# A hybrid SSD, sparse-attention and mixture-of-experts step on one core: squares after the gates, attention in double steps, and a reworked residual stage

## The reference

```python
h = rmsnorm(x, norm_g);  proj = h @ w_in          # z, xBC, dt, q, k, v, indexer, two gates
y_ssd = ssd_scan(silu(causal_conv(xbc)), ...)     # 4 groups of heads, chunks of 64
y_ssd = rmsnorm(y_ssd * silu(z), ssm_norm_g)      # its squares are summed over all 2048 channels
branch_a = y_ssd @ w_ssm_out
o = dsa_attention(q, k, v, indexer ...)           # 16 heads, 2 KV heads; scores masked to the top keys
branch_b = o @ w_attn_out
x = x + (sigmoid(g0) * branch_a + sigmoid(g1) * branch_b) @ w_o      # the residual stage
h = rmsnorm(x);  group and expert logits -> 2 experts of one group of 8, out of 32
for e in range(32):
    he = silu(h @ w1[e]) * (h @ w3[e]);  y += combine[:, e] * (he @ w2[e])
out = rmsnorm(x + y)
```

## Time and profile before

| | us |
|---|---|
| runs: median (lowest to highest) | 1581.36 (1580.76 to 1584.17) |
| the profiled execution | 1584.12 |
| its span, first to last instruction | 1582.5 |
| PE busy, DVE, ACT, POOL | 1428.0, 659.1, 470.7, 177.9 |
| from the end of `ga` (688.5) to the first scores (734.8) | 46.3 |
| prompt attention (734.8 to the first scores of the running streams, 826.45) | 91.65 |
| last x1 half read (1258.2) to the first expert's transposes (1290.87) | 32.6 |
| first to last scatter of the experts' results (1308.3 to 1547.2) | 238.9 |

### The profile page before, as it was taken

The page is one execution under the profiler, slowest core; times in us unless marked ns, Lnnn a source line. Parts: engine busy times, 40 slices in busy tenths (PEclk is TensorE's granted clock), DMA queues, the critical chain, the costliest instruction groups (busy, mean ns, idle before and its releaser), DMA issues.

```text
span 1582.5 us, 19000 instructions
## 1 busy us (share of the span) xinstructions
PE 1428.0 (90%) x7458; PEld 893.7 (56%) x7458; DVE 659.1 (42%) x1467; ACT 470.7 (30%) x1059; POOL 177.9 (11%) x270
## 2 busy tenths in 40 slices
PE   7999999999999999979988899999999949878780
PEld 5545654754754745756555677777765535544440
DVE  3059952775785785602755521000023523211105
ACT  2161025643643743413765500000002111111112
POOL 3000000310221221220000000000000013222210
PEclk9999999999999999988999999999999959999986
DMA  7721314423523423525008520212033199999975
GB/s 230 217 80 29 107 54 122 160 98 93 171 87 106 158 87 102 161 99 149 15 14 170 148 110 0 106 53 53 20 136 128 56 381 394 415 415 416 414 292 206
DMA packets 135180, 247.43 MB, mean 156 GB/s; under 512 B 38836, under 2 KB 81572, under 8 KB 126164
## 3 DMA queue, kind: packets, MB, share of 16 engines
q1 hardware_dynamic: 124020, 215.10, 39.8%
q0 software_dynamic: 11072, 31.12, 5.5%
HBM read 216.50 MB, written 36.88 MB: 160 GB/s over the span
## 4 chain that ended last, share of the span: by engine, by line
PE 82%; ACT 5%; DVE 5%; DMA 4%; issue 3%; POOL 1%; SPq 1%; DVEq 0%; ACTq 0%; POOLq 0%
PE psum L1262 49%; PE psum L1536 8%; PE psum L1266 5%; PE psum L1440 4%; PE psum L1552 3%; ACT arena L1721 2%; PE psum L1294 2%; PE psum L1182 1%; ACT arena L1798 1%; PE psum L1172 1%; PE psum L1247 1%; DMA x_rows<-oT 1%; PE psum L1075 1%; DVE arena L2423 1%; PE psum L1211 1%
## 5 line engine op out<-in xcount | busy, mean ns | idle before, releaser
L1262 PE MATMUL psum<-hT,wring 128*128 128x512 f32 (+2 forms) x2176 | 597.1, 436 | 0.4 <-issue 0.4
L1262 PEld LDWEIGHTS psum<-hT,wring 128*128 128x128 f32 x2176 | 350.3, 192 | 237.3 <-issue 197.1
L1266 PE MATMUL psum<-ident,arena 128*128 128x128 f32 (+3 forms) x950 | 143.1, 288 | 40.3 <-DMA arena<-x_rows,src_row 16.9
L1721 ACT ACTIVATE arena<-psum 128x512 f32<-128x512 f32 (+9 forms) x199 | 106.8, 578 | 204.7 <-PE psum L1262 138.0
L1266 PEld LDWEIGHTS psum<-ident,arena 128*128 128x128 f32 (+3 forms) x950 | 106.6, 145 | 98.2 <-issue 78.1
L1262 PE MATMUL psum<-arena,wring 128*128 128x320 f32 x512 | 138.1, 431 | 0.0
L1262 PEld LDWEIGHTS psum<-arena,wring 128*128 128x128 f32 x512 | 96.6, 189 | 41.2
L1536 PE MATMUL psum<-wring,arena 128*64 128x256 f32 x608 | 78.7, 417 | 25.2 <-issue 20.1
L1536 PEld LDWEIGHTS psum<-wring,arena 128*64 128x64 f32 x608 | 51.4, 151 | 48.0 <-issue 29.1
L2430 DVE TENSOR_TENSOR arena<-psum,arena 128x128 f32<-128x128 f32 x32 | 9.3, 292 | 161.3 <-ACT arena L1865 152.6
L2359 DVE TENSOR_TENSOR arena<-psum,arena 128x320 f32<-128x320 f32 x16 | 7.9, 491 | 156.1 <-PE psum L1262 156.1
(11 more groups left out here) (318 smaller groups left out, 1504.8 us busy)
## 6 DMA issues: line engine op xcount, KB each, us to landing
wring<-in_w SPq DMA_DIRECT2D x38, 1024.0 KB
arena<-in_w SPq DMA_DIRECT2D x32, 1024.0 KB
wring<-in_w_in SPq DMA_DIRECT2D x13, 2048.0 KB, 7.9
hT<-in_w SPq DMA_DIRECT2D x14, 1024.0 KB
oT<-in_w SPq DMA_DIRECT2D x12, 1024.0 KB
arena<-a_rows SPq DMA_DIRECT2D x20, 512.0 KB, 4.3
arena<-in_state_ssm SPq DMA_DIRECT2D x16, 512.0 KB, 7.3
out<-arena POOLq DMA_DIRECT2D x16, 512.0 KB, 4.2
```

The source lines that it names most:

```text
L1262: ins = mm(out, chunk[:, k, m0:m0 + m], rhs(k), start=first and k == 0, stop=last and k == ks - 1)
L1266: return nc.tensor.transpose(out, in_, ident[0:rows, 0:rows])
L1721: release(fn(out, in_, ACT.Copy), key)
```

## The change

1. `squares_pe` moves behind `gb`.
2. Prompt attention takes two pairs per step d: scores of 2d and 2d+1, values of the two pairs of step d-2, transposes of the two of step d-1. A transposed head has one bank of a pool of three (4, 5, 6), "o" has bank 7 alone. The multiplication by the reciprocal goes to POOL (64 instructions, L957 of the new file), DVE keeps the reciprocal and copies head 1's transposes (L2087), ACT copies head 0's. `sm` has 8 buffers for 6, `pT` 4 for 2.
3. Residual stage: x is loaded for all five tiles at once, straight into x1, and added in place; `h2T` keeps two tiles and `xn` three, in other memory than oT. So w13(0), w2(0), w13(1) and w13(2) are issued right behind x. After the last x1 half come w2(1), w13(3), w2(2); w13(4), w2(3), w2(4) come when the last router is done, the rows are stored and the first gather has landed. For the last tile, its second transposes and its `scale` stand ahead of the picks of tile 3; ranks and places of tile 3 stand behind the picks of tile 4. The memset of `rows_in` moves up behind the first store.

```diff
@@ def plan_group / ssd_pe
-                    if j == 3:
-                        squares_pe(pe, g)
                 w = wait_chunk(pe, ("wgb", 0))
...
+                squares_pe(pe, g)
@@ def attention_pe
+            for d in range(PAIRS // 2 + 2):
+                for stage, lag in ((scores, 0), (values, 2), (probs_turned, 1)):
+                    for m in (2 * (d - lag), 2 * (d - lag) + 1):
+                        if 0 <= m < PAIRS:
+                            stage(m)
@@ plan_banks
+        if d >= 2 and d % 2 == 0:
+            b.add(("o", (d - 2) // 2), (7,))
+        for a in range(2):
+            if 1 <= d < PAIRS // 2 + 1:
+                for g in range(AKV):
+                    b.add(("pT", 2 * d - 2 + a, g), (4, 5, 6))
@@ POOL
+            for u in range(AKV * PAIRS):
+                w = P * (u // AKV // AR + 1)
+                pool.wait_ge(S["rinv_ready"], u + 1)
+                nc.gpsimd.tensor_tensor(sm[:, u % 8, 0:w], sm[:, u % 8, 0:w],
+                                        rinv[:, u % 8:u % 8 + 1].broadcast_to([P, w]), ALU.mult).then_inc(S["p_scaled"], 1)
@@ attention_dve, per double step, behind four least()
+                for a in range(2):
...
+                            nc.vector.reciprocal(rinv[:, u % 8:u % 8 + 1], rsum[:, u % 8:u % 8 + 1]) \
+                                .then_inc(S["rinv_ready"], 1)
+                    if 0 <= m < PAIRS:
...
+                        release(copy(pT[:, a, 1, 0:w], bank(key)[:, 0:w]), key)
@@ SP
-                sp.dma_start(xres[:, tt % 2, :], src).then_inc(pair["xres_loaded"][tt % 2], 16)
-                if tt == 1:
-                    load13(0)
-                    load13(1)
+                sp.dma_start(x1[:, tt, :], src).then_inc(tile_loaded[tt], 16)
+            load13(0)
+            load2(0)
+            load13(1)
+            load13(2)
             wait_read(sp, ("x1", NT - 1, 1))
-            load2(0)
-            load13(2)
             load2(1)
             load13(3)
             load2(2)
             wait_full(sp, ("rt", NT - 1))
+            rows_stored(sp)
+            sp.wait_ge(gathered_rows[0], 16)
+            load13(4)
             load2(3)
-            sp.wait_ge(S["xn_stored"], 16 * NT)
-            load13(4)
             load2(4)
@@ residual, and the ring of h2T, on DVE
                 release(tt_(x1[:, t, 512 * m:512 * m + 512], bank(("x1", t, m)),
-                            xres[:, t % 2, 512 * m:512 * m + 512], ALU.add), ("x1", t, m))
+                            x1[:, t, 512 * m:512 * m + 512], ALU.add), ("x1", t, m))
+                if t >= 2:
+                    wait_full(dve, ("rt", t - 2))
@@ the last tile on DVE (PE has the same shape with rows_turned, ranked, placed)
-                if tt > 0:
+                if 0 < tt < NT:
                     turned_rows(tt - 1, 1)
                     scale(tt - 1)
...
+                if tt == NT - 1:
+                    turned_rows(tt, 1)
+                    scale(tt)
                 if tt > 0:
                     select_dve(dve, tt - 1, link)
+            place_dve(dve, NT - 2, link)
             place_dve(dve, NT - 1, link)
```

More of the change, by code:

```diff
@@ L161, in plan_banks @@
         plan_group(b, g)
[L162 to L169, removed]
+    for d in range(PAIRS // 2 + 2):
+        for a in range(2):
+            if d < PAIRS // 2:
+                for g in range(AKV):
+                    b.add(("s", 2 * d + a, g), (0, 1, 2, 3))
+        if d >= 2 and d % 2 == 0:
+            b.add(("o", (d - 2) // 2), (7,))
+        for a in range(2):
+            if 1 <= d < PAIRS // 2 + 1:
+                for g in range(AKV):
+                    b.add(("pT", 2 * d - 2 + a, g), (4, 5, 6))
     for s in range(-1, SB + 1):
@@ L271, in plan_group @@
                 b.add(("gb", 0, c, h), lo)
+        for i in range(2):
+            b.add(("ss", g, i), hi)
 def hybrid_layer(nc, x_prompt, x_sample, cache_k, cache_v, cache_kidx, state_conv, state_ssm,
@@ L459, in hybrid_layer @@
         a5 = Arena(arena, KD * T)
-        xres, x1 = a5.take(2, D), a5.take(NT, D)
-        h2T, xn = a5.take(KD, T), oTf.rearrange("p (t d) -> p t d", t=NT)
+        w2_first, x1 = a5.take(2 * D), a5.take(NT, D)
+        h2T, xn = a5.take(2, KD, P), a5.take(3, D)
         rows_in, hgT, ysl = a5.take(RS, HD2), a5.take(2, KD, SLOTS), a5.take(RS, HD2)
@@ L562, in hybrid_layer, with rows_stored @@
         pair = {name: [sem(f"{name}{i}") for i in range(2)] for name in (
-            "kx_loaded", "kb_loaded", "bexp_loaded", "vb_loaded", "xres_loaded", "cin_loaded")}
+            "kx_loaded", "kb_loaded", "bexp_loaded", "vb_loaded", "cin_loaded")}
+        xn_stored = [sem(f"xn_stored{i}") for i in range(3)]
+        def rows_stored(eng):
+            for i in range(3):
+                eng.wait_ge(xn_stored[i], 16 * len(range(i, NT, 3)))
         def final_sp(sp, r):
@@ new lines, in scores, with values @@
+            def scores(n):
+                i, t = n // AR, n % AR
+                for g in range(AKV):
+                    o = claim(pe, ("s", n, g))
+                    rows = slice(HD * g, HD * (g + 1))
+                    filled(mm(o[:, 0:P * (i + 1)], oT[rows, t, i * P:(i + 1) * P], kT[rows, 0:P * (i + 1)],
+                              start=True, stop=True), ("s", n, g))
+            def values(m):
+                i, t = m // AR, m % AR
+                if m % 4 == 0:
+                    claim(pe, ("o", m // 4))
+                oo = bank(("o", m // 4))
+                for g in range(AKV):
+                    wait_read(pe, ("pT", m, g))
+                for c in range(i + 1):
+                    for g in range(AKV):
+                        ins = mm(oo[HD * g:HD * (g + 1), (t % 4) * P:(t % 4 + 1) * P],
+                                 kvtm[:, c, SV + g * HD:SV + (g + 1) * HD], pT[:, m % 2, g, c * P:(c + 1) * P],
+                                 start=c == 0, stop=c == i)
+                if m % 4 == 3:
+                    filled(ins, ("o", m // 4))
```

171 lines of the change are left out of this document (82 added, 89 removed).

## The result

| | before | changed |
|---|---|---|
| median of four runs each, us | 1582.25 (1580.76 to 1584.17) | 1555.86 (1555.1 to 1556.15) |
| profiled execution, its span | 1584.12, 1582.5 | 1556.15, 1554.4 |

The ratio is 0.983, with a 95% interval of 0.982 to 0.985: 26.4 us less, where 30.0 were forecast. The time lies in the range, and the forecast case holds. The forecast's 1551.4 was counted down from 1581.4, the median of three of these four runs of before. Each 0.001 of a ratio is 1.6 us here. The three terms of the forecast came out unequally well.

The account below looks back on a forecast made before the run. PE bounds the kernel where it waits, runs at the lower clock or is fed by DMA, which bounds the experts. Gains of 10.5 + 8.4 + 11.1 = 30.0 us from 1581.4 give 1551.4 us, range 1541 to 1565.

Parts of the forecast that it names:

- the forecast case: Whole kernel: the three gains sum to 30.0 us, giving 1551.4 us; chance 0.60.
- Squares: Between the gates: idle time goes, gb and the ones' matmuls run at full clock; gain 10.5 us, bounds 8.3 and 11.5.
- Attention: Prompt attention: double steps take 83.3 us for 91.65, a gain of 8.4; bounds a loss of 5, a gain of 12.
- the second limit: Prompt attention: four transposed heads share three banks, so the fourth waits for ACT's copy of the first, behind four exponents.
- 19.1 for four at 384: Prompt attention: four double steps at width 384 take 19.1 us (4.3, 4.95, 4.8, 5.05).
- 3.8 + 4.35 at 256: Prompt attention: two double steps at width 256, the second longer because ACT copies "o" (0.57 us) first.
- POOL's products at nothing: Prompt attention: POOL's products, 1.043 us at 512 columns, have nearly a step before their transpose, so they cost nothing.
- Rival 2: Prompt attention: POOL is too slow, products of 2 us sharing SBUF access with DVE; 13 us back, 1565 us; chance 0.07.
- Experts: Residual stage and experts: 12.6 us of bytes moved ahead, plus 5.5, less 6.7 of idle; gain 11.4, taken as 11.1.
- The two idle terms: Experts' DMA: 6.7 us of new idle time before the first gather lands, against 5.5 regained, mostly from 1296 to 1308.
- Rival 1: Prompt attention: the clock does not fall, or for a shorter time; 3.3 us more gain, 1548 us; chance 0.13.
- Rival 3: Expert stage gives little: first gather takes 7.7 us or lists come later; 5 to 9 back, 1556 to 1560; chance 0.15.

Follow-up runs that it names:

- act_order: The changed kernel with ACT copying the first transposed head ahead of its fourth exponent in each double step, outputs of four pairs last; 1542.39 us, ratio 0.976.
- late_prefetch: The changed kernel with w2(0) and w13(2), 3.15 MB, issued behind the last x1 half again; 1556.19 us, ratio 0.983.

## Why the prediction was right, and where it was not

- **Squares, 10.5 forecast, 10.7 in the traces, 10.4 by undoing.** Each step of it held: no gap, ones' matmuls 0.87 on the chain for the 1.3 taken, full clock. The one thing not seen is DVE's two copies of the sums (0.70 and 0.29 us), which now stand ahead of the first minimum.
- **Attention, 8.4 forecast, 6.9 in the traces, 6.6 by undoing.** The mechanism that I named as the second limit, the fourth transpose behind ACT's copy of the first, is the one that bounds the stage, and act_order shows it. Mis-sized, for 2.5 us in all: "19.1 for four at 384" took 20.8, 3.8 + 4.35 at 256 took 8.5, and 24.4 at 512 took 24.8; against that the steps at the lower clock took 17.0 for 18.0. The fill and tail came out right. What I missed is what the limit said: that it could be moved by the order of ACT's queue, for 6.1 us or more.
- **POOL's products at nothing: right.** They take 1.01 to 1.04 us beside a DVE full of minima, which take 0.69 us at 512 before and after, and the wait that the chain puts on them at 512 went away with ACT's order while they stayed as they were. Rival 2 falls. The forecast gave the second half of the Trainium skill's rule (GPSIMD Engine Reference, Key points) without its condition: the page says that GpSimd shares its SBUF interfaces with VectorE, and ties the contention to VectorE instructions in a 2-port perf mode or with two SBUF inputs. DVE's minima read one input from PSUM (`arena<-psum,arena`), so that sentence does not foretell products of 2 us beside them, and at 1.04 us in the SSD stage and 1.01 to 1.04 here no run shows a cost. The first half, that VectorE is the engine for such work (Engine selection), agrees on the single product (0.49 for 1.04); on the stage, DVE with the products took 0.7 us more.
- **Experts, 11.1 forecast, 8.3 in the trace, 8.9 by undoing.** The times of the steps were near: gather issued at 17.2 for 16.3 (POOL's issue comes 1.06 us behind the lists), flight 3.45 for 2.5, an idle stretch of 7 us as forecast. The bytes came out as forecast too: summed over the windows of the stage, DMA moves 105.1 MB after the last half for 110.3 before, 5.2 MB or 12.4 us at 415 GB/s. The two idle terms, forecast together at 6.7 - 5.5 = 1.2 us of loss, came to 1.7: in the first 60 us behind the half DMA moves 345 GB/s for 357 before, 0.7 MB less. That makes 10.7, and U fell by 10.0. What is missing from 11.1 in the trace is mostly the last `up`, 5.36 us for 3.67, which no term had and which came in five of fourteen traces; that part of the miss is chance. What the forecast's form hides is that the terms are not separate gains: bytes fetched ahead are worth little where DMA would idle anyway (late_prefetch, 1.3 to 1.9 us for 3.15 MB), and an early store is worth more where the queue is long.
- **Rival 1** (a clock that does not fall) was priced at 3.3 us. It was not forced in the changed kernel; in act_order, with 7 us of lower clock, it gave 1.5. **Rival 3** did not come true: the gather did not take 7.7 us and the lists were 0.9 us late. That 1555.9 lies close to its 1556 to 1560 has other reasons, 1.5 us missing in attention and the last `up`.

## What to carry to other kernels

When a pool of buffers is smaller than a step's demand, put the read that frees the first buffer ahead of unrelated work in the reader's queue, and reads that nobody waits for last: here such a reordering gave at least 6.1 us, and 9.9 with a clock that came back sooner. Where the profile names an engine as releaser, check which of its instructions the waiter needs; if that one was long done, look for another that ends at the same time. Where DMA bounds a stage, add the bytes left to move and the idle time of DMA, and change both together: bytes fetched ahead that would have filled a hole of DMA are worth almost nothing. Before a difference of 2 us is given to a change, look whether the last pieces of work ran at the same clock in both traces.

## What the runs showed of the hardware

- The granted clock fell in every run whose fill-in left PE its gaps (PE busy for 2.10 of 4 us in the changed kernel, for 2.58 and 3.14 in act_order, ahead of the fall and over it), and stayed at 1.00 with 2.4 us of useless matmuls in them. Once fallen, it stayed at 0.50 for 7 to 20 us, although from the third of these us on PE was busy for 3.5 to 4.0 of each 4 us; for the same code of attention it stayed for 14 us in three runs and for 17 in four.
- The same last `up` of 32 records took 3.67 us in nine traces and 5.36, at a lower granted clock, in five, three of seven with the same code from the residual stage on.
- A float32 matmul counts as two in the record: the fillers of 128x512 took 0.99 us each (1.98 for two, x4), where I had read 0.43 from a row whose 16 are eight products.
- The same 64-row gather flew 3.1 to 3.6 us on an idle DMA and 6.3 to 7.7 among weights; a row store of 0.5 MB took 8.5 to 8.6 us with 4 or 7 MB of weights issued ahead of it or with it, 13.2 to 13.5 with 8.
